# More ConvFFN columns by seven products, and two of their weight sums made by accumulating DMAs

## The reference, cut to what matters

```python
def conv_ffn(h, prefix, w_up, conv_w, conv_b, w_down):
    up = h @ w_up                                    # 1024 -> 2 * 2816
    c, new_state = causal_dwconv(up, prefix, conv_w, conv_b)
    g, u = c[..., :D_FF], c[..., D_FF:]
    return (jax.nn.silu(g) * u) @ w_down, new_state  # 2816 -> 1024
...
  x += ConvFFN(RMSNorm(x))
```

## Time and profile before

| what | us |
|---|---|
| median of 3 runs (range) | 864.27 (863.23 to 864.78) |
| the profiled execution | 864.73 |
| its span, first to last instruction | 862.9 |
| TensorE busy | 844.2 (98%) |
| VectorE busy | 555.5 (64%) |
| ScalarE busy | 395.3 (46%) |
| GpSimd busy | 120.6 (14%) |

### The profile page before, as it was taken

One profiled execution on the slowest core, in us unless ns is written; L12 is line 12 of the kernel. 1 busy time (PEld: TensorE's weight loads), 2 busy tenths in 40 slices (PEclk: granted clock), 3 DMA queues, 4 the chain that ended last, 5 costly groups with the idle time before them and its releaser, 6 DMA issues.

```text
span 862.9 us, 17433 instructions
## 1 busy us (share of the span) xinstructions
PE 844.2 (98%) x6836; PEld 794.9 (92%) x6836; DVE 555.5 (64%) x981; ACT 395.3 (46%) x704; POOL 120.6 (14%) x181
## 2 busy tenths in 40 slices
PE   7999999999999999999999999999999999999995
PEld 7998878789999999877899999999999999999995
DVE  6444246678584642465445799799599599597754
ACT  7302133366353621354333666465455465365352
POOL 2320000000000000000000321223223142131200
PEclk9999999999999999999999999999999999999998
DMA  9798699721233474579223434764764665463523
GB/s 310 252 359 302 209 335 335 252 87 42 71 99 99 154 257 175 173 259 383 90 92 97 161 103 125 160 140 110 128 156 103 113 172 113 92 145 78 194 74 104
DMA packets 55187, 144.62 MB, mean 168 GB/s; under 512 B 6499, under 2 KB 9063, under 8 KB 54466
## 3 DMA queue, kind: packets, MB, share of 16 engines
q1 hardware_dynamic: 48496, 128.86, 45.0%
q0 software_dynamic: 6320, 14.53, 9.8%
q10 hardware_dynamic: 290, 0.12, 0.1%
HBM read 125.35 MB, written 18.14 MB: 166 GB/s over the span
## 4 chain that ended last, share of the span: by engine, by line
PE 81%; DVE 2%; issue 1%; ACT 1%; DMA 1%; DVEq 0%; SPq 0%; ACTq 0%
PE proj L1204 47%; PE score L1286 3%; PE score L1287 3%; PE score L1288 3%; PE proj L1160 3%; PE proj L1221 2%; PE T L1288 2%; PE T L1286 2%; PE T L1287 2%; PE proj L1223 2%; PE proj L1222 2%; PE score L1455 2%; PE score L1421 1%; PE T L1297 1%; PE T L1440 1%
## 5 line engine op out<-in xcount | busy, mean ns | idle before, releaser
L1204 PE MATMUL proj<-a_hi,w_hi 128*128 128x272 f32 (+1 forms) x740 | 160.0, 291 | 8.0 <-DVE w_lo L1922 6.0
L1555 ACT ACTIVATE w_hi<-w_raw 128x1024 fp32r<-128x1024 f32 (+2 forms) x120 | 110.9, 925 | 112.9 <-PE proj L1204 86.7
L1204 PE MATMUL proj<-a_lo,w_hi 128*128 128x272 f32 (+1 forms) x740 | 158.5, 289 | 0.0
L1204 PE MATMUL proj<-a_hi,w_lo 128*128 128x272 f32 (+1 forms) x740 | 158.0, 288 | 0.0
L1899 DVE TENSOR_TENSOR w_lo<-w_raw,w_hi 128x1024 fp32r<-128x1024 f32 (+2 forms) x120 | 126.8, 1060 | 42.6 <-ACT w_hi L1555 42.3
L1204 PEld LDWEIGHTS proj<-a_hi,w_hi 128*128 128x128 f32 x740 | 118.5, 189 | 14.9 <-issue 7.6
L1204 PEld LDWEIGHTS proj<-a_lo,w_hi 128*128 128x128 f32 x740 | 119.1, 190 | 0.0
L1204 PEld LDWEIGHTS proj<-a_hi,w_lo 128*128 128x128 f32 x740 | 118.5, 190 | 0.0
L1136 POOL COPY f_state<-up_pad 128x18 f32<-128x18 f32 x44 | 45.7, 1039 | 156.2 <-DVE up_pad L2055 156.2
L1204 PE MATMUL proj<-d_hi,w_hi 128*128 128x272 f32 x320 | 66.0, 287 | 0.0
L1204 PE MATMUL proj<-d_hi,w_lo 128*128 128x272 f32 x320 | 65.8, 288 | 0.0
(11 more groups left out here) (364 smaller groups left out, 1906.5 us busy)
## 6 DMA issues: line engine op xcount, KB each, us to landing
x<-in_w_up SPq DMA_DIRECT2D x24, 512.0 KB, 4.6
w_raw<-in_w_in SPq DMA_DIRECT2D x21, 512.0 KB, 4.0
w_raw<-in_w_up SPq DMA_DIRECT2D x20, 512.0 KB, 3.6
early_pages<-in_cache_k SPq DMA_DIRECT2D x32, 256.0 KB, 6.0
pages<-in_cache_v SPq DMA_DIRECT2D x32, 256.0 KB, 5.5
c_pages<-in_cache_mem_k SPq DMA_DIRECT2D x16, 512.0 KB, 6.9
c_pages<-in_cache_mem_v SPq DMA_DIRECT2D x16, 512.0 KB, 6.4
w_raw<-in_w_down SPq DMA_DIRECT2D x32, 256.0 KB, 2.7
```

The source lines that it names most:

```text
L1204: mm = pe.matmul(tile_banks(n)[:, half, 0:width], wt, act[:, at, half * HALF:half * HALF + width], start=(k == 0 and a == 0), stop=(k == w ...
L1555: act.activation(w_hi[:, n % W_HI_RING, 0:kt, :], w_raw[:, n % W_RING, 0:kt, :], ACT.Copy).then_inc(w_hi_ready, 1)
```

## The change

The set of columns that are computed by products grows from 12 (5-7, 9-11, 13-15, 17-19) to 15 (5-7 and 9-20). The down tiles of groups 0 to 3 are dealt in twos to columns 4-7 and 9-20, where they were with columns 4-19; column 8 has none now, and column 20 has two. Two of the four sums of weight blocks are not made by VectorE any more. A third load on SP's queue brings the first half of the up block into `t_raw[0]`, and two DMAs that GpSimd issues (`pair_join`) add rows of the gate block to `p_raw[1]` and to `t_raw[0]` in place. For this the signs are turned: the blends of the activations are formed with other signs, and the gate half of the result is multiplied by -1 where it is scaled (`up_in`). ScalarE's split of `p_raw[1]` and VectorE's `sums` wait for both added DMAs; a load into the area waits for the sums before. `sums` now stands behind product 7 in VectorE's order, where it stood ahead of the second down tile. `x_back` is moved from the end of column 20 to column 21, behind its gate tile.

```diff
@@ -41,3 +41,3 @@
 FFN_GROUPS = [range(0, 4), range(4, 8), range(8, 12), range(12, 16), range(16, 22)]
-PAIRED = [i for i in range(5, 20) if i % 4]
+PAIRED = [i for i in range(5, 21) if i != 8]
 DIST = 384
@@ -91,5 +91,7 @@
 
-    g = next(g for g, group in enumerate(FFN_GROUPS) if i in group)
-    j = i - FFN_GROUPS[g][0]
-    return [(f"down{g - 1}", "add", n) for n in (2 * j, 2 * j + 1)] if g and j < 4 else []
+    hosts = [c for c in range(4, 21) if c != 8]
+    if i not in hosts:
+        return []
+    g, j = divmod(hosts.index(i), 4)
+    return [(f"down{g}", "add", n) for n in (2 * j, 2 * j + 1)]
 
@@ -352,3 +354,3 @@
         p = PAIRED.index(prev)
-        nearer = [("pair_split", q, 1)], [("pair_hi", q, 2), ("pair_split", q, 2), ("pair_load", q + 1, 1)]
+        nearer = [("pair_split", q, 1)], [("pair_hi", q, 2), ("pair_split", q, 2), ("pair_load", q + 1, 1), ("pair_load", q + 1, 2)]
         ahead, behind = nearer if q < len(PAIRED) else ([], [])
@@ -372,5 +374,5 @@
             s += [("prod", q, 5), ("prod", q, 6), ("pair_out", q, 5), ("add", downs[0]), ("pair_out", q, 6)]
-            s += [("sums", q + 1)] * more + [("act", i - 1)] * prev_paired
-            s += [("tile", downs[1])] + hi1 + lo1 + [("pair_hi", q + 1, 0)] * more
-            s += [("prod", q, 7), ("pair_out", q, 7), ("add", downs[1])] + [("pair_split", q + 1, 0)] * more
+            s += [("act", i - 1)] * prev_paired
+            s += [("tile", downs[1])] + hi1 + lo1 + [("pair_hi", q + 1, 0), ("pair_join", q + 1)] * more
+            s += [("prod", q, 7), ("pair_out", q, 7), ("add", downs[1])] + [("pair_split", q + 1, 0), ("sums", q + 1)] * more
             s += [("prod", q, 3)] + [("pair_hi", q + 1, 1)] * more + [("pair_out", q, 3), ("up_in", i, 0), ("prod", q, 4)]
@@ -383,2 +385,4 @@
             s.append(("norm", "up"))
+        if i == FT - 1:
+            s.append(("x_back",))
         if prev_paired:
@@ -388,5 +392,9 @@
         elif i + 1 == PAIRED[0]:
-            s += hi0 + hi1 + [("up_in", i, 0)] + lo0 + lo1 + [("pair_load", 0, 0), ("pair_load", 0, 1), ("blend_lo", i - 1), ("taps", i, 0)]
-            s += [("sums", 0), ("tile", up_tile), ("pair_hi", 0, 0), ("pair_hi", 0, 1), ("up_in", i, 1), ("pair_split", 0, 0), ("pair_load", 1, 0)]
-            s += [("pair_hi", 0, 2), ("pair_split", 0, 1), ("taps", i, 1), ("pair_split", 0, 2), ("pair_load", 1, 1), ("gate", i)]
+            s += hi0 + hi1 + [("up_in", i, 0)] + lo0 + lo1 + [("pair_load", 0, j) for j in range(3)] + [("blend_lo", i - 1), ("taps", i, 0)]
+            s += [("tile", up_tile), ("up_in", i, 1), ("pair_hi", 0, 0), ("pair_split", 0, 0), ("pair_join", 0)]
+            s += [("taps", i, 1), ("pair_hi", 0, 1), ("gate", i)]
+            (hi0, lo0), (hi1, lo1) = (split_next(f) for f in downs)
+            s += [("tile", downs[0])] + hi0 + lo0 + [("add", downs[0]), ("sums", 0), ("pair_load", 1, 0), ("pair_hi", 0, 2), ("tile", downs[1])] + hi1 + lo1
+            s += [("add", downs[1]), ("pair_split", 0, 1), ("pair_split", 0, 2), ("pair_load", 1, 1), ("pair_load", 1, 2), ("act", i)]
+            continue
         else:
@@ -400,4 +408,2 @@
                 s.append(("blend", i))
-        if i == FT - 2:
-            s.append(("x_back",))
         for f in downs:
@@ -773,2 +779,6 @@
 
+        def wait_joined(eng, q):
+
+            eng.wait_ge(sem("lams_and_joins_landed"), 80 + 32 * (q + 1))
+
         def wait_x_free(eng):
@@ -991,6 +1001,11 @@
                         wait_pair_lo(sp, arg - 1, j)
+                        sp.wait_ge(sem("sums_made"), arg)
                     else:
                         wait_x_free(sp)
-                    sp.dma_start(p_raw[:, j, :, :], t["w_up"][((D_FF, 0)[j] + PAIRED[arg] * P) // P, :, :, :]
-                                 ).then_inc(sem(f"slot_landed1_{j}"), 16)
+                    if j < 2:
+                        sp.dma_start(p_raw[:, j, :, :], t["w_up"][((D_FF, 0)[j] + PAIRED[arg] * P) // P, :, :, :]
+                                     ).then_inc(sem(f"slot_landed1_{j}"), 16)
+                    else:
+                        sp.dma_start(t_raw[:, 0, :, :], t["w_up"][(D_FF + PAIRED[arg] * P) // P, :, 0:4, :]
+                                     ).then_inc(sem("slot_landed1_2"), 16)
                 if kind == "x_store":
...
@@ -1124,2 +1139,8 @@
                                    ).then_inc(sem(f"x_added{m % 2}"), 16)
+                if kind == "pair_join":
+                    gate_rows = t["w_up"][PAIRED[arg]]
+                    pool.wait_ge(sem("slot_landed1_1"), 16 * (PAGE_AREA.count(1) + arg + 1))
+                    pool.dma_start(p_raw[:, 1, 0:4, :], gate_rows[:, 4:8, :], accum_op=ALU.add).then_inc(sem("lams_and_joins_landed"), 16)
+                    pool.wait_ge(sem("slot_landed1_2"), 16 * (PAGE_AREA.count(1) + arg + 1))
+                    pool.dma_start(t_raw[:, 0, :, :], gate_rows[:, 0:4, :], accum_op=ALU.add).then_inc(sem("lams_and_joins_landed"), 16)
                 if kind == "taps":
@@ -1845,2 +1866,4 @@
                         act.wait_ge(sem("slot_landed1_0"), 16 * (PAGE_AREA.count(1) + q + 1))
+                    elif part == 1:
+                        wait_joined(act, q)
                     else:
...
@@ -2053,5 +2076,11 @@
                         mine, few, taken = prompt_of(proj[n % 2][:, :, :]), samples_of(proj[n % 2][:, :, :]), tile_out[n % 2]
-                    dve.tensor_tensor(by_half(pad[:, 2:2 + SEQ]), mine, prompt(rstd), ALU.mult).then_inc(sem("up_in"), 1)
-                    dve.tensor_tensor(free_dims(pad, 4 + SEQ, [(6 * GB, 2), (6, GB), (1, DEC_SEQ)]), few, samples(rstd),
-                                      ALU.mult).then_inc(taken, 1)
+                    mine_to, few_to = by_half(pad[:, 2:2 + SEQ]), free_dims(pad, 4 + SEQ, [(6 * GB, 2), (6, GB), (1, DEC_SEQ)])
+                    if i in PAIRED and j == 0:
+                        dve.scalar_tensor_tensor(out=mine_to, in0=mine, scalar=-1.0, in1=prompt(rstd), op0=ALU.mult,
+                                                 op1=ALU.mult).then_inc(sem("up_in"), 1)
+                        dve.scalar_tensor_tensor(out=few_to, in0=few, scalar=-1.0, in1=samples(rstd), op0=ALU.mult,
+                                                 op1=ALU.mult).then_inc(taken, 1)
+                    else:
+                        dve.tensor_tensor(mine_to, mine, prompt(rstd), ALU.mult).then_inc(sem("up_in"), 1)
+                        dve.tensor_tensor(few_to, few, samples(rstd), ALU.mult).then_inc(taken, 1)
                 elif kind == "taps":
@@ -2082,7 +2111,9 @@
                     dve.wait_ge(sem("xw_ready"), 2 * arg + 2)
-                    side(dve.tensor_tensor(e[:, 0, :], xw[:, 0, two], xw[:, 1, two], ALU.add))
-                    settle()
                     side(dve.tensor_tensor(e[:, 2, :], xw[:, 0, one], xw[:, 0, two], ALU.subtract))
-                    done(dve.tensor_tensor(e[:, 1, :], xw[:, 0, one], e[:, 0, :], ALU.subtract))
-                    dve.tensor_tensor(e[:, 3, :], xw[:, 1, one], e[:, 1, :], ALU.add).then_inc(sem("blend_raw"), 1)
+                    settle()
+                    side(dve.tensor_tensor(e[:, 0, :], xw[:, 1, two], xw[:, 0, two], ALU.subtract))
+                    done(dve.scalar_tensor_tensor(out=e[:, 1, :], in0=e[:, 2, :], scalar=-1.0, in1=xw[:, 1, two],
+                                                  op0=ALU.mult, op1=ALU.subtract))
+                    dve.scalar_tensor_tensor(out=e[:, 3, :], in0=e[:, 1, :], scalar=-1.0, in1=xw[:, 1, one],
+                                             op0=ALU.mult, op1=ALU.subtract).then_inc(sem("blend_raw"), 1)
                 elif kind == "blend_lo":
@@ -2095,8 +2126,5 @@
                         dve.wait_ge(sem(f"slot_landed1_{j}"), 16 * (PAGE_AREA.count(1) + arg + 1))
-                    one, two = slice(0, 4), slice(4, 8)
-                    b11, b21, b12, b22 = (p_raw[:, j, ks, :] for j in range(2) for ks in (one, two))
-                    side(dve.tensor_tensor(t_raw[:, 0, :, :], b12, b11, ALU.subtract))
-                    settle()
-                    side(dve.tensor_tensor(b12, b22, b12, ALU.subtract))
-                    done(dve.tensor_tensor(t_raw[:, 1, :, :], t_raw[:, 0, :, :], b22, ALU.subtract))
+                    wait_joined(dve, arg)
+                    b21, b22 = (p_raw[:, j, 4:8, :] for j in range(2))
+                    done(dve.tensor_tensor(t_raw[:, 1, :, :], t_raw[:, 0, :, :], b22, ALU.add))
                     dve.tensor_tensor(t_raw[:, 2, :, :], t_raw[:, 1, :, :], b21, ALU.add).then_inc(sem("sums_made"), 1)
```

More of the change, by code:

```diff
@@ L1028, in _ @@
             pool.dma_start(rel[0:BUCKETS, :], t["rel_bias"]).then_inc(sem("bias_loaded"), 16)
-            pool.dma_start(row_cols[:, :], t["const_rows"]).then_inc(sem("lams_loaded"), 16)
+            pool.dma_start(row_cols[:, :], t["const_rows"]).then_inc(sem("lams_and_joins_landed"), 16)
             for j, name in enumerate(("lambda_q1", "lambda_k1", "lambda_q2", "lambda_k2")):
@@ L1032, in _ @@
```

(11 more changed lines are left out.)

## The result

The changed kernel takes 898.73 us (median of 6 runs, 895.2 to 904.01); the kernel before, on the same chip, takes 864.48 (863.23 to 864.93). The ratio is 1.0402, with a 95% interval of 1.0386 to 1.0418. The forecast was 872, so its sign was right and its size was not, and the time lies outside the range. The profiled execution has a span of 896.0 us and a time of 898.2; of before they were 862.9 and 864.7.

The account below looks back on a forecast made before the run. TensorE was taken to bound the ConvFFN. Span 862.9 - 4.5 (matmuls) + 12.35 (late `t_lo`, 13 x 0.95) = 870.8, 872.6 with the 1.8 around it, less 0.5 for the median, called 872; range 858.5 to 887 us.

Parts of the forecast that it names:

- What is removed, 4.5 us: TensorE in columns 12, 16 and 20: 36 matmuls leave at 0.125 us each, saving 4.5 us.
- Step 1: Tile A's result: ScalarE's copies keep their order, so GpSimd's add still follows the start of product 5 by 2.9 us.
- Step 2: GpSimd's queue: both joins stand right behind tile A's add, 0.85 us per issue, their loads already landed.
- Step 3: Landing of the joins: add after 4.4 us, 1.65 us per join, 0.4 for a down tile's load; second lands at 656.0.
- Step 4: VectorE from the joins' landing to `t_lo`, with hand-over to TensorE: 6.5 us, so `t_lo` comes 0.95 us late.
- The sum of a column: Paired column behind a paired one: about 17.5 us instead of 16.55, 0.95 us late in each of 13 columns.
- The entry: From column 4 into the first paired column: two waits lost, `t_lo` late by about as much; 0, ends -1.9 and +2.
- Column 8 and `x_back`: Plain column 8 without down tiles, VectorE catching up in column 9, and `x_back` moved with the last add: no cost, 0.
- the fourth one: Rival: joins land one after the other without overlap, or slowed by loads; 2 to 4.4 us per column, 886 to 917; chance 0.08.
- The first: Rival: joins land in time, by 655.07, so only the 36 matmuls count; 859.8 us, or 857.9; chance 0.30.
- the estimate by the fit of the Trainium skill: GpSimd's joins: about 2.0 us plus bytes at 436 GB/s, so 262 KB lands after 2.6 us and costs nothing.

Follow-up runs that it names:

- experiment 2: Changed kernel with both accumulating DMAs (the joins) left out, VectorE and ScalarE waiting for the slots' loads instead; 859.2 us, ratio 0.9948.
- experiment 8: Kernel before with the 15 product columns, new down-tile dealing and moved `x_back`, all four sums on VectorE, no joins or signs; 859.9 us, ratio 0.9946.
- experiment 10: Kernel of experiment 8 with column 4's sums and gate moved back behind `up_in` and tile A's weight halves; 858.95 us, ratio 0.9935.
- experiment 5: Changed kernel with the previous column's gate step (ScalarE's silu, VectorE's product) moved behind the copy of tile A; 881.61 us, ratio 1.0185.
- experiment 9: Kernel of experiment 1 with ScalarE's gate silu in column 4 moved ahead of its second `p_hi`; 864.88 us, ratio 1.0004.
- experiment 6: Changed kernel with 16 filler matmuls ahead of product 5 in each paired column behind a paired one; 900.6 us, ratio 1.0405.
- experiment 1: Changed kernel with GpSimd's two joins issued ahead of its add of tile A instead of behind it; 865.93 us, ratio 1.0022.

## Why the prediction was wrong, step by step

- **What is removed, 4.5 us: right.** Experiments 2, 8 and 10 gain 5.1, 4.3 and 5.1 us.
- **Step 1 failed.** It says that the add of tile A follows product 5 by 2.9 us, "the order of these is not changed". The order is the same, but what releases it is not. Ahead of the copy on ScalarE stands the silu, behind taps that VectorE makes only after `t_lo`. As long as `t_lo` was early this didn't show; once it is late, it delays the add too: R + 3.85 on average in columns 9 to 19, so 0.92 us more per column. The silu's part is 0.72, read where nothing else is in the way (columns 10, 12, 14 and 16), and experiment 5 shows it. The rest is mainly TensorE at half clock in columns 11, 13 and 15, and column 9, where the add comes at R + 4.50, and with the silu moved still at R + 4.38. In the forecast the delay was carried from column to column by product 5 alone, which is one of the two ways.
- **Step 2: right in its order, too slow by a little.** The joins are issued 0.55 and 1.09 us behind the add, not 0.85 and 1.75.
- **Step 3 was sized too low.** From the add's issue to the sums behind the joins it takes 8.74 us on average in columns 9 to 19, against 8.05: 0.69 more. The add landed 4.43 us after its issue, as forecast; the first join landed 2.10 us behind the add, where I had 1.65; the second 2.09 behind the first, where I had 1.65 and 0.4 for the load; the sums began 0.12 later. So the term that failed is above all the 1.65 us for the first join, 0.45 of the 0.69. One error in it is a wrong count: I gave an add 128 packets, but it has 144, as the queue shows around the single add of rows 9 (647.9 to 652.4 us in the kernel before):

```profile
q0 software_dynamic: 144, 0.28, 50.1%
```

  With 144 the same row gives 4.0 x 144 / 264 = 2.18 us and a least of 1.62, not 1.94 and 1.44, and 2.1 lies between them. GpSimd's queue from 662 to 664 us in the changed kernel has 167 packets in 2.0 us, 1.72 us for the 144 of a join:

```profile
q0 software_dynamic: 167, 0.31, 102.2%
```

  In these 2 us the queue filled the DMA engines by itself. Behind them it shared them with SP's load of a down tile (256 KB, issued at 662.16, landed 5.2 us later), here from 664 to 667 us:

```profile
q1 hardware_dynamic: 144, 0.26, 23.2%
```

  The load held 23.2% of 3 us, 0.70 us, where I had counted 0.4; yet the second join took no more than the first, so its 2.09 us do not tell the two parts apart. With the silu moved (experiment 5) the joins landed 2.07 and 1.75 us behind one another and the whole step was 8.2. Why the second one lands sooner there stays open. Tile B's add, next in the same queue, comes 4.2 to 4.8 us behind tile A's in columns 10 to 16 of the changed kernel and 4.8 to 4.9 there; no run takes it away.
- **Step 4: right.** From the sums to the next product 5 it takes 6.32 us, forecast 6.5.
- **The sum of a column:** 17.48 forecast, plus 0.92, plus 0.69, less 0.18 is 18.91, as measured. The lateness is 2.36 and not 0.95 us, in eleven columns, and the first group behaves alike.
- **The entry failed.** I took 0 with an upper end of 2; it is 3.5. The joins were issued at 530.2 as forecast but held ScalarE until 537.7, not 536, and ScalarE's and VectorE's weight halves queue behind that (experiment 9).
- **Column 8 and `x_back`: right in themselves.** 1.6 and about 1 us came in place of 0, but as half clock behind the waits of columns 7 and 20 (experiment 6), a term that the forecast did not have. Experiments 1 and 2 have `x_back` in the same place and take 70.1 us from R of column 20 to the end, the changed kernel 71.7.
- **The rivals.** By its time (2.36 per column, 886 to 917) the fourth one, held for 0.08, came true, but not by its reason: the joins did overlap. The first failed, and with it the estimate by the fit of the Trainium skill (DMA: Bandwidth & Descriptors, "Anatomy of one DMA — SWDGE (gpsimd) path"), 2.6 us for 256 KB from GpSimd. A plain copy in this place took 5.0 and an accumulating one 7.6, both in a queue with others. The load that agreed with the fit (2.6 us) was issued by SP, not by GpSimd.

## What to carry to other kernels

When an instruction is put behind another in a queue, its delay is passed on by every path that leads back to the one ahead of it, not only by the bottleneck engine: follow the loop until it closes, with the new wait taken as late, and its length is the time of an iteration. When a transfer is priced by its packets, count those of a whole transfer first. Issue a transfer that nothing holds up ahead of one that waits for a late result. And before work is taken off an engine, look whether anything waits for that engine; here nothing did at 45 of 50 us busy.
